# Adding the experts' outputs to token rows in DRAM by an accumulating DMA, in place of matmuls that add them to the residual in SBUF

## The reference

```
def moe_swiglu(h, w_router, w_gate, w_up, w_down):
    logits = (h @ w_router).astype(jnp.float32)
    top_val, top_idx = lax.top_k(logits, TOP_K)
    wts = jax.nn.softmax(top_val, axis=-1)
    gates = jnp.sum(jax.nn.one_hot(top_idx, N_EXPERTS, dtype=jnp.float32) * wts[..., None], axis=-2)
    y = jnp.zeros(h.shape, jnp.float32)
    for e in range(N_EXPERTS):
        y = y + gates[..., e:e + 1] * swiglu(h, w_gate[e], w_up[e], w_down[e]).astype(jnp.float32)
    return y.astype(h.dtype)
```

## Time and profile before

| what | value |
|---|---|
| median of 3 runs | 1963.39 us (1959.56 to 1963.56) |
| the profiled execution, its time | 1959.33 us |
| its span | 1957.5 us |
| busy: PE / DVE / ACT / POOL | 92% / 67% / 48% / 5% |
| moved by DMA | 517.63 MB, 264 GB/s over the span |
| expert loop, from its first matmul to the last | 944.3 to 1931.5 us |

### The profile page before, as it was taken

The page is one execution under the profiler, slowest core; times in us unless marked ns, Lnnn a source line. Parts: engine busy times, 40 slices in busy tenths (PEclk is TensorE's granted clock), DMA queues, the critical chain, the costliest instruction groups (busy, mean ns, idle before and its releaser), DMA issues.

```text
span 1957.5 us, 27112 instructions
## 1 busy us (share of the span) xinstructions
PE 1807.6 (92%) x9907; PEld 1496.2 (76%) x9907; DVE 1315.8 (67%) x1371; ACT 938.8 (48%) x824; POOL 88.2 (5%) x106
## 2 busy tenths in 40 slices
PE   6999798899999985677999999999999999999996
PEld 4788793799999652346788888888888888888885
DVE  5863875354543332004588888888888888898895
ACT  3542000144432021102577777777777777777773
POOL 1340303000000000000000000000000000000000
PEclk8998796899999999787899999999999999999998
DMA  7222002455554879993499999999999999999991
GB/s 285 108 93 87 1 1 94 153 194 183 183 176 147 270 242 386 343 405 123 183 364 373 359 362 373 347 368 356 359 376 345 367 359 354 376 345 368 359 346 61
DMA packets 98236, 517.63 MB, mean 264 GB/s; under 512 B 10985, under 2 KB 11114, under 8 KB 45922
## 3 DMA queue, kind: packets, MB, share of 16 engines
q1 hardware_dynamic: 81936, 478.50, 65.0%
q10 hardware_dynamic: 13970, 25.46, 3.6%
q0 software_dynamic: 2240, 12.49, 1.8%
HBM read 508.11 MB, written 8.30 MB: 264 GB/s over the span
## 4 chain that ended last, share of the span: by engine, by line
PE 78%; issue 9%; DVE 6%; ACT 2%; ACTq 2%; SPq 1%; DMA 1%; POOLq 0%; POOL 0%; DVEq 0%
PE bank L975 14%; PE bank L977 14%; PE bank L976 14%; PE bank L492 5%; PE bank L493 5%; PE bank L494 5%; PE bank L725 3%; PE bank L791 3%; PE bank L703 1%; PE bank L604 1%; PE bank L648 1%; PE bank L969 1%; PE bank L1014 1%; PE bank L628 1%; ACTq L405 1%
## 5 line engine op out<-in xcount | busy, mean ns | idle before, releaser
L1799 DVE TENSOR_TENSOR w_lo<-raw_w,w_hi 128x2048 fp32r<-128x2048 f32 x336 | 768.8, 2290 | 120.7 <-ACT w_hi L1237 116.4
L1237 ACT ACTIVATE w_hi<-raw_w 128x2048 fp32r<-128x2048 f32 x336 | 644.9, 1920 | 362.9 <-PE bank L977 273.5
L975 PE MATMUL bank<-w_hi,xe_hi 128*128 128x512 f32 x896 | 364.9, 407 | 1.5 <-DVE xe_lo L1860 1.5
L977 PE MATMUL bank<-w_hi,xe_lo 128*128 128x512 f32 x896 | 350.1, 391 | 0.0
L976 PE MATMUL bank<-w_lo,xe_hi 128*128 128x512 f32 x896 | 349.5, 390 | 0.0
L493 PE MATMUL bank<-fh_lo,w_hi 128*128 128x264 f32 x704 | 201.6, 286 | 0.0
L977 PEld LDWEIGHTS bank<-w_hi,xe_lo 128*128 128x128 f32 x896 | 168.5, 188 | 36.1
L975 PEld LDWEIGHTS bank<-w_hi,xe_hi 128*128 128x128 f32 x896 | 168.6, 188 | 35.9 <-issue 1.8
L976 PEld LDWEIGHTS bank<-w_lo,xe_hi 128*128 128x128 f32 x896 | 168.8, 188 | 33.7
L975 PE MATMUL bank<-w_hi,aT_hi 128*128 128x512 f32 x448 | 176.7, 394 | 0.0
L977 PE MATMUL bank<-w_hi,aT_lo 128*128 128x512 f32 x448 | 174.7, 390 | 0.0
(11 more groups left out here) (340 smaller groups left out, 2283.2 us busy)
## 6 DMA issues: line engine op xcount, KB each, us to landing
raw_w<-in_moe SPq DMA_DIRECT2D x336, 1024.0 KB, 4.8
raw_w<-in_ffn_w SPq DMA_DIRECT2D x42, 1024.0 KB, 4.8
ring<-in_k_pages SPq DMA_DIRECT2D x96, 256.0 KB, 3.6
raw_w<-in_gdn_in SPq DMA_DIRECT2D x16, 1024.0 KB, 6.8
ring<-in_v_pages SPq DMA_DIRECT2D x64, 256.0 KB, 11.3
ring<-in_v_pages ACTq DMA_DIRECT2D x64, 256.0 KB, 10.9
ring<-in_att_in SPq DMA_DIRECT2D x4, 2048.0 KB, 7.9
ring<-in_k_pages ACTq DMA_DIRECT2D x32, 256.0 KB, 7.0
```

Source lines behind the costliest of these rows:

```text
L975: mm(out, hi, move_hi, start=first, stop=False)
L977: return mm(out, lo, move_hi, start=False, stop=last)
L1237: A(w_hi[:, p % SPLIT, :], raw_w[:, p % RAW, :], ACT.Copy).then_inc(split_hi, 1)
L1799: V.tensor_tensor(w_lo[:, p % SPLIT, :], raw_w[:, p % RAW, :], w_hi[:, p % SPLIT, :].bitcast(F32), ALU.subtract).then_inc(split_lo, 1)
```

## The change

The results of the experts no longer come back through PE and DVE. A second buffer in DRAM, `y_dram`, holds a row for each token and 128 more for slots that have no token. POOL zeroes it ahead of the loop. `number_slots` multiplies `pick` with two columns instead of one (`tok_gate`: the token number and the gate), so that each slot has its gate beside its row number; it now also runs for expert 0. ACT scales by the gate as it copies the output to `ye`, and POOL issues an indirect DMA that adds the 128 rows of `ye` to their rows of `y_dram` (`add_rows`). DVE keeps row numbers and gates of the running expert in a second pair of tiles (`slot_put`, `gate_put`, at its piece 12), since those of the next are computed meanwhile. After the last expert's addition has landed, POOL reads the 264 rows back into `htok` (`sums_back`), PE turns them (`turn_sums`, 3 transposes for each feature tile), and DVE adds them to `xT` as before. `spread`, `pick_g` and the combines inside the loop are gone.

```diff
+        h_dram = nc.dram_tensor("h_dram", [T + CAP, D], F32, kind="Internal").ap()
+        y_dram = nc.dram_tensor("y_dram", [T + CAP, D], F32, kind="Internal").ap()
...
-                    last = mm(bank[0][:, 0:1], pick[:, i, :], tok_no[:, i:i + 1], start=(i == 0), stop=(i == 2))
+                    last = mm(bank[0][:, 0:2], pick[:, i, :], tok_gate[:, i, :], start=(i == 0), stop=(i == 2))
                 last.then_inc(slot_ps, 1)
...
-            def combine(v, d):
-
-                if d == 0:
-                    pe.wait_ge(ye_sb, v * 2 + 2)
+            def turn_sums(d):
+
                 if d >= 2:
-                    pe.wait_ge(comb_added, v * KT + (d - 1))
-                mm(bank[4 + d % 2][:, 0:T], ye[:, P * d:P * (d + 1)], spread, start=True, stop=True).then_inc(comb, 1)
+                    pe.wait_ge(comb_added, d - 1)
+                for i, (t0, n) in enumerate(TOK_TILES):
+                    last = nc.tensor.transpose(bank[4 + d % 2][:, t0:t0 + n], htok[0:n, i, P * d:P * (d + 1)], ident[0:n, 0:n])
+                last.then_inc(comb, 1)
...
-                        if p == UP_PIECES:
-                            pe.wait_ge(spread_sb, v + 1)
+                        if p == UP_PIECES and not first:
+                            pe.wait_ge(ye_sb, v * 2)
...
-                    if not first and 5 <= p < 5 + 2 * KT and p % 2 == 1:
-                        combine(v - 1, (p - 5) // 2)
...
-                    if p == 24:
-
-                        if not first:
-                            pe.wait_ge(comb_added, v * KT)
-                        for i, (t0, n) in enumerate(TOK_TILES):
-                            last = nc.tensor.transpose(bank[4][0:CAP, t0:t0 + n], pick_g[0:n, i, :], ident[0:n, 0:n])
-                        last.then_inc(spread_ps, 1)
...
             gather(0)
+            number_slots(0)
             expert(0, first=True)
...
             with pe.If(over_cap == 0):
+                pe.wait_ge(tok_rows, H_ROWS + 16 * NE + Y_TILES)
                 for d in range(KT):
-                    combine(NE - 1, d)
+                    turn_sums(d)
...
             def take_y(v):
                 act.wait_ge(piece_used, v * PIECES + PIECES)
+                act.wait_ge(put_set, v + 1)
+                act.wait_ge(y_rows, v * 16 + Y_CLEAR)
                 for half in range(2):
-                    A(ye[:, N * half:N * (half + 1)], bank[4 + half][:, :], ACT.Copy).then_inc(ye_sb, 1)
+                    A(ye[:, N * half:N * (half + 1)], bank[4 + half][:, :], ACT.Copy, scale=gate_put).then_inc(ye_sb, 1)
...
             pool.wait_ge(h_tok, 6)
-            pool.wait_ge(slot_set, 1)
+            link(G.memset(ye, 0.0))
             for i, (t0, n) in enumerate(TOK_TILES):
-                pool.dma_start(h_dram[1 + t0:1 + t0 + n, :], htok[0:n, i, :]).then_inc(tok_rows, 16)
-            pool.dma_start(h_dram[0:1, :], htok[32:33, 2, :]).then_inc(tok_rows, 16)
-            pool.wait_ge(tok_rows, 64)
+                pool.dma_start(h_dram[t0:t0 + n, :], htok[0:n, i, :]).then_inc(tok_rows, 16)
+                pool.dma_start(y_dram[t0:t0 + n, :], ye[0:n, :]).then_inc(y_rows, 16)
+            pool.dma_start(h_dram[T:T + CAP, :], ye).then_inc(tok_rows, 16)
+            pool.dma_start(y_dram[T:T + CAP, :], ye).then_inc(y_rows, 16)
...
+            def add_rows(v):
+
+                pool.wait_ge(put_set, v + 1)
+                pool.wait_ge(ye_sb, 2 * v + 2)
+                G.indirect_dma_start(y_dram, bass.IndirectOffsetOnAxis(ap=slot_put[:, 0:1], axis=0), ye, None,
+                                     compute_op=ALU.add).then_inc(y_rows, 16)
+
+            def sums_back(experts):
+
+                pool.wait_ge(gathered, 2 * experts + 2)
+                pool.wait_ge(y_rows, Y_CLEAR + 16 * experts)
+                for i, (t0, n) in enumerate(TOK_TILES):
+                    pool.dma_start(htok[0:n, i, :], y_dram[t0:t0 + n, :]).then_inc(tok_rows, 16)
+
+            for v in range(NE):
+                fetch(v + 1)
+                add_rows(v)
...
             def pick_tokens(v):
 
                 at_v = slice(v, v + 1) if isinstance(v, int) else bass.ds(v, 1)
-                for i, (t0, n) in enumerate(TOK_TILES):
-                    V.tensor_scalar(pick_g[0:n, i, :], c_("slot_no")[0:n], rpos[0:n, i, at_v], rgate[0:n, i, at_v],
-                                    ALU.is_equal, ALU.mult)
+                V.tensor_copy(tok_gate[:, 0:2, 1:2], rgate[:, 0:2, at_v])
+                V.tensor_copy(tok_gate[0:NS, 2, 1:2], rgate[0:NS, 2, at_v])
+                V.tensor_tensor(tok_gate[:, :, 0:1], tok_less[:, :].unsqueeze(2), rpos[:, :, at_v], ALU.subtract)
+                for i in range(3):
                     last = V.tensor_scalar(pick[:, i, :], c_("slot_no"), rpos[:, i, at_v], None, ALU.is_equal)
...
-                    if not first and 9 <= p < 9 + 2 * KT and p % 2 == 1:
-                        add_combined(v - 1, (p - 9) // 2)
+                    if p == 12:
+                        if not first:
+                            dve.wait_ge(y_rows, v * 16 + Y_CLEAR)
+                        V.tensor_copy(gate_put, gate_tok)
+                        V.tensor_copy(slot_put[:, :], slot_tok[:, :]).then_inc(put_set, 1)
...
             pick_tokens(0)
+            slots(0)
+            dve.wait_ge(slot_set, 1)
             rest_of_gathered(0)
```

More of the change, by code:

```diff
@@ L170, in program @@
         slot_tok = sb("slot_tok", [P, 1], I32)
-        tok_no = sb("tok_no", [P, 3])
-        h_dram = nc.dram_tensor("h_dram", [1 + T, D], F32, kind="Internal").ap()
+        slot_put = sb("slot_put", [P, 1], I32)
+        tok_gate = sb("tok_gate", [P, 3, 2])
+        slot_col = sb("slot_col", [P, 3])
+        tok_less = sb("tok_less", [P, 3])
+        empty_row, gate_tok, gate_put = (slot_col[:, i:i + 1] for i in range(3))
+        h_dram = nc.dram_tensor("h_dram", [T + CAP, D], F32, kind="Internal").ap()
+        y_dram = nc.dram_tensor("y_dram", [T + CAP, D], F32, kind="Internal").ap()
         bank = [ctx.enter_context(nc.psum_tensor(f"bank{i}", [P, 512], F32))[:, :] for i in range(8)]
@@ L1041, in _ @@
                         expert(e + NE * rnd)
+                pe.wait_ge(tok_rows, H_ROWS + 16 * ROUNDS * NE + Y_TILES)
                 for d in range(KT):
-                    combine(ROUNDS * NE - 1, d)
+                    turn_sums(d)
             norm_sums(4)
@@ L1282, in expert @@
                             .then_inc(aT_hi_set, 1)
-                    if p == UP_PIECES:
-                        act.wait_ge(spread_ps, v + 1)
-                        A(spread, bank[4][0:CAP, 0:T], ACT.Copy).then_inc(spread_sb, 1)
                     if p == PIECES - 1:
@@ L1378, in fetch @@
                     .then_inc(tok_rows, 16)
-            for v in range(1, NE + 1):
-                fetch(v)
-            over_cap = pool.value_load(more[0:1, 0:1], min_val=0, max_val=1)
-            with pool.If(over_cap == 1):
-                for v in range(NE + 1, ROUNDS * NE + 1):
-                    fetch(v)
+            def add_rows(v):
[11 more added lines that the diff above has]
+                add_rows(v)
+            over_cap = pool.value_load(more[0:1, 0:1], min_val=0, max_val=1)
+            with pool.If(over_cap == 0):
+                sums_back(NE)
+            with pool.Else():
+                for v in range(NE, ROUNDS * NE):
+                    fetch(v + 1)
+                    add_rows(v)
+                sums_back(ROUNDS * NE)
             pool.wait_ge(normed, 5 * KT)
@@ L1827, in _ @@
             dve.wait_ge(pos_ps, 1)
-            V.memset(htok[32:33, 2, :], 0.0).then_inc(slot_set, 1)
+            link(V.memset(tok_gate[:, :, :], 0.0))
             for i in range(3):
-                V.tensor_scalar(tok_no[:, i:i + 1], bank[0][:, 96:97], float(P * i), None, ALU.add)
+                V.tensor_scalar(tok_less[:, i:i + 1], bank[0][:, 96:97], float(P * i - 1 - T), None, ALU.add)
+            V.tensor_scalar(empty_row, bank[0][:, 96:97], float(T - 1), None, ALU.add)
             link(V.memset(rpos, -1.0))
@@ L1862, in rest_of_gathered, with slots, add_combined @@
                 last.then_inc(xe_lo_set, 1)
-            def add_combined(v, d):
-                dve.wait_ge(comb, v * KT + (d + 1))
+            def slots(v):
+                dve.wait_ge(slot_ps, v + 1)
+                V.tensor_copy(gate_tok, bank[0][:, 1:2])
+                V.tensor_scalar(slot_tok[:, :], bank[0][:, 0:1], empty_row, None, ALU.add).then_inc(slot_set, 1)
+            def add_combined(d):
+                dve.wait_ge(comb, d + 1)
                 V.tensor_tensor(xT[:, d, :], xT[:, d, :], bank[4 + d % 2][:, 0:T], ALU.add).then_inc(comb_added, 1)
@@ L1889, in expert @@
                     if p == UP_PIECES:
-                        dve.wait_ge(spread_ps, v + 1)
+                        dve.wait_ge(slot_ps, v + 1)
                         dve.wait_ge(gathered, v * 2 + 2)
@@ L1893, in expert @@
                     if p == 34:
```

(11 more changed lines are left out.)

10 lines of the change are left out of this document (6 added, 4 removed).

## The result

| | before | after |
|---|---|---|
| median | 1961.93 us (1959.56 to 1963.56, 4 runs) | 1945.28 us (1943.88 to 1948.70, 4 runs) |
| the profiled execution, its time | 1959.33 us | 1944.25 us |
| its span | 1957.5 us | 1942.5 us |
| first expert matmul to `ye` of the last expert | 988.32 us | 956.92 us |
| `ye` of the last expert to the end of the span | 24.9 us | 40.3 us |

The ratio is 0.9915, with a 95% interval of 0.9901 to 0.9929: 0.85% faster, where 0.8% was forecast. The profiled execution took 1944.25 us; the sum of the steps gave 1944.2.

A forecast was written before the change was run, and what follows sets the result against it. PE was taken to bound the expert loop: -30.0 in it, +1.0 ahead and +13.9 behind sum to -15.1 us, from 1959.33 to 1944.2. As a median 1948.3 us was forecast, range 1944 to 1954 (chance 0.58).

The forecast's parts named there:

- What bounds the loop, and its gain: Expert loop: PE is never idle, so removing 56 combines (25.5 us) and the turned gates (4.5 us) saves 30.0 us.
- The turned gates: In the expert loop: removing them saves PE 0.56 us in each of eight experts, 4.5 us.
- The additions cost the loop nothing: In the expert loop: weights, fetch and addition fit the DMA engines with 7 to 9% to spare, so no cost.
- The room: In the loop: DMA engines have 5.1 MB, or 12 us of all engines, to spare per expert.
- Ahead of the loop: Before the first expert matmul: 0.8 us less before PE's gather, 1.8 more behind it, net +1.0 us (-0.5 to +2.5).
- Behind the loop: After the last `ye`: POOL's start 0.3, addition 8.0 and reads 4.6 us add a wait of 13.0 us.
- The turned sums and the clock: At the end: turned sums +0.1 us with DVE setting the pace, low PE clock on sums of squares +0.8.
- The bounds: Whole kernel: unknown costs give 1943.5 to 1957 us; parts of rivals 1 and 3 raise the upper end to 1960.
- the slow addition (1): At the end: addition takes 12 to 20 us to land, loop untouched; 1953.5 us at 13.2, 1960.3 at 20; chance 0.14.
- The late weights (2): In the loop: additions hold DMA engines and weights come late; 1964 us at 13.5 us each, 1976 at 15; chance 0.06.
- the loop not bound by PE (3): In the loop: weights or splitting chain set the pace; 1973.8 us in full (0.05), 1952 to 1962 in part (0.09).
- Less at the end (4): At the end: addition lands in 5 us or the clock stays up, giving 1943 to 1946 us; chance 0.08.

The follow-up runs named there:

- run 1: Kernel before without the 56 combines in the loop and DVE's additions of them, nothing in their place: 1934.06 us, ratio 0.986.
- run 2: Kernel before without the 56 loop combines and also without the turned gates of experts 1 to 7: 1926.20 us, ratio 0.9825.
- run 5: Changed kernel with four additions per expert for experts 0 to 6, three into arrays nobody reads: 1950.31 us, ratio 0.9943 to before.
- run 7: Changed kernel with expert 0's row numbers written behind the `xe_lo` operations, numbered in their own bank: 1943.59 us, ratio 0.9904 to before.
- run 8: Changed kernel with 56 matmuls of no use in PE's wait for the sums at the end: 1944.68 us, ratio 0.9912 to before.
- runs 3 to 8: Changed kernel with plain write (1942.77 us), two additions (1948.26), four (1950.31), unaltered (1944.33), expert 0's row numbers later (1943.59), useless matmuls at the end (1944.68).
- run 9: Changed kernel with the last expert combined by matmul, experts 0 to 6 through DRAM, expert 0's row numbers behind `xe_lo`: 1932.94 us, ratio 0.9851 to before.

## Why the prediction was right, point by point

- **What bounds the loop, and its gain.** Right. 31.4 us measured for 30.0; run 1 gives the 56 combines 26.4 for 25.5. The second column in the numbering of slots, priced at nothing, cost nothing: PE's distance around it is 1.25 to 1.26 us with one column and with two.
- **The turned gates**: the one term of the loop that was mis-sized. In the earlier trace rows I compared the place with them to one with turned activations alone and read 0.56 us each. Run 2 gives 0.76. Those rows lie in two experts, and show only the distance at the place itself. The other 0.2 us falls four pieces later, around the transposes of the activations at piece 28, which go faster once the gates are gone. Why they do, no run here shows; ACT's copy of `spread` and PE's wait for it, both at piece 28, went together with the gates.
- **The additions cost the loop nothing.** Right within 0.1 us each (run 2 against after). The room was overrated: I had 12 us, and with four additions, 10.6 us, PE already waits (run 5). The price per addition was not worked out at all; it is 2.6 us of all engines.
- **The limit of about 358 GB/s** of the Trainium skill ("DMA: Bandwidth & Descriptors", Specifications), set aside for the rows: 379 GB/s over the whole of expert 1, 386 with four additions, 425 for 10 us. Setting it aside was right. The same page of the Trainium skill, section Bandwidth, says that its figure is what each of two cores gets when both stream, and that one core alone gets more; this kernel runs on one core.
- **Ahead of the loop**: +1.0 forecast, of which -0.8 before the gather and +1.8 behind it. Measured -1.5 and +1.65; run 7 confirms the second. In the first the clearing alone gave 0.85, and the three wide picks 0.6 more, so my 0.8 left one of the two out. The step as a whole cost +0.2. PE's numbering took 1.44 us where I had 1.2.
- **Behind the loop**: 13.0 us for the wait; 13.5 measured. The parts are less good than their sum: the addition came back to POOL after 7.1 us for my 8.0, POOL began 0.76 us after `ye` where I had 0.3, and the reads took 5.7 us for my 4.6, since three issues at 0.6 us follow each other and each read takes 4.2 to 4.6 us to land, for which I had taken a write's 3.4.
- **The turned sums and the clock**: +0.9 forecast, +1.2 measured, but for another reason. I took DVE for the pace of the turned sums and put the low clock's cost on the sums of squares. The granted clock was 0.50 throughout 1915 to 1928 and PE set the pace: 0.82 us a tile for 0.69 (run 8). The sums of squares took no longer than before, as their first half had been at the low clock there too. The store of `y` took 0.7 us more, which I had not counted; no run here says why.
- **The sum.** -15.1 forecast, -15.0 between the spans, but that near only by luck: the loop gave 1.4 us more than forecast, the way from the router to it 2.1 more (0.8 the step itself, 1.3 the clock on the small matmuls), the end took 1.5 more, and 2.1 us came from the router's later start. Without that start it would be -17.1.
- **The median.** I set the median 4.1 us above the profiled execution, as in the runs shown of before. A fourth run of before brought its median down to 1961.93, 2.6 above, and after's is 1.0 above. That is the 3.0 us between 1948.3 and 1945.28.
- **The bounds.** By their own terms they come to 1944.1 and 1957.7 and not to 1943.5 and 1957; nothing else hangs on these.

The rivals: the slow addition (1) fell, at 7.1 us; in the loop it did take 11.4, where no one waits for it. The late weights (2) and the loop not bound by PE (3) fell to runs 2 and 1. Less at the end (4) fell too: the addition landed after 6.6 us and the clock was low.

## What to carry to other kernels

Read a bound engine's gain from the distance between its starts, and then look for the place where the replacement is *not* hidden: here 56 combines became free in the loop, but the last addition, with nothing to stand behind, took back half. Use the new way where it is covered and keep the old one for the last step; this made 0.6% more than the change itself. For a DMA keep two prices apart, the engines' time that it takes (it decides beside a full stream) and what it takes to land (it decides where one waits). And compare two traces between marks that the change doesn't touch: the start of the loop alone differed by 5 us between executions, and the slow start of expert 0 in run 1 would put 0.13 us too much on each turned gate.

## What the runs showed of the hardware

- An accumulating indirect DMA of 128 rows of 4 KB takes 2.6 us of all 16 DMA engines beside the weights and 3.3 to 3.7 alone at the end, a plain write 1.3 in both places (runs 3 to 8). It lands after 6.0 to 6.6 us on idle engines (write 3.5) and 11.4 us beside a stream of 379 GB/s (write 9.3).
- While it runs, all DMA together falls to 294 GB/s for 5 us, where the same 5 us of run 2, which has no additions, have 383; in the 20 us after that it runs at 421 to 425 GB/s. Seven buffers of 1 MB hide this from PE with one addition and with two; with four PE waits up to 1.0 us at a time (three wasn't tried).
- Issuing it costs POOL 1.57 us on idle engines and 1.86 in the loop, a plain indirect write 0.97 and 1.25.
- ACT's copy of 128x512 from PSUM with a scale per partition takes 0.68 us in after, a plain one 0.59; the two halves of `ye` 1.27 for 1.08.
- PE's granted clock was 0.50 from its first matmul after 15 us without work, through 13 us in which it worked for 9.5, and back at 1.00 at 1929. In run 9, where only 1.3 us without work stood before its first matmul, it was 1.00 throughout the same steps.
